# Attention in pairs of maps and modulation on two column tiles, in a two-layer diffusion trunk on one core

## The reference, cut to what matters

```python
mod = silu(c) @ w_mod[l] + b_mod[l]            # c and c_ctx; w_mod[l] is 1024 x 6144
shift1, scale1, gate1, shift2, scale2, gate2 = split(mod, 6)
h = rms_norm(x) * (1 + scale1) + shift1
q, k, v of three groups = h @ w_in[l]
#  A: 6 heads, window attention with a bias, plus context keys
#  B: 4 heads, two softmax maps each, p0 - lambda * p1
#  C: 6 query heads on 2 key heads
x = x + gate1 * (concat(softmax(q k) v) @ w_out[l])
h2 = rms_norm(x) * (1 + scale2) + shift2
x = x + gate2 * peer_ffn(h2)                   # 8 heads, top 16 of 16384 experts, for every token
```

## Time and profile before

| | |
|---|---|
| time, median of 3 runs | 5093.09 us (5086.49 to 5101.38) |
| the profiled execution | 5102.09 us, of it span 5100.3 us |
| PE busy | 75% of the span |
| DVE, ACT, POOL busy | 55%, 28%, 27% |
| mean granted TensorE clock | 0.924 |
| attention, layers 0 and 1 | 327.9 to 641.7 us, 2833.3 to about 3147 us |
| experts, layer 0 | 916.7 to about 2600 us |

### The profile page before, as it was taken

The page is one execution under the profiler, slowest core; times in us unless marked ns, Lnnn a source line. Parts: engine busy times, 40 slices in busy tenths (PEclk is TensorE's granted clock), DMA queues, the critical chain, the costliest instruction groups (busy, mean ns, idle before and its releaser), DMA issues.

```text
span 5100.3 us, 42883 instructions
## 1 busy us (share of the span) xinstructions
PE 3820.1 (75%) x14332; PEld 1753.3 (34%) x14332; DVE 2829.5 (55%) x6023; ACT 1444.8 (28%) x4223; POOL 1398.6 (27%) x1477
## 2 busy tenths in 40 slices
PE   7787779887777777777767776867777777777776
PEld 1364436222222222323234544432222222222222
DVE  2443365665675766745455334556657567575444
ACT  1224422222223222222222334222222222322222
POOL 1001200233343333433320111003333334333332
PEclk9886779999999999999988758989999999999999
DMA  7210012999999999999951000119999999999997
GB/s 253 72 40 1 1 54 73 389 407 406 417 414 416 416 406 413 401 416 401 418 188 50 15 1 17 63 68 410 412 412 416 411 419 406 420 416 395 406 419 290
DMA packets 214077, 1460.21 MB, mean 286 GB/s; under 512 B 23968, under 2 KB 24224, under 8 KB 49248
## 3 DMA queue, kind: packets, MB, share of 16 engines
q0 software_dynamic: 186496, 1355.11, 65.1%
q1 hardware_dynamic: 27360, 102.37, 5.9%
HBM read 1453.19 MB, written 4.19 MB: 286 GB/s over the span
## 4 chain that ended last, share of the span: by engine, by line
PE 41%; DMA 37%; DVE 12%; ACT 6%; issue 4%; SPq 0%; POOL 0%; ACTq 0%; DVEq 0%; POOLq 0%
DMA work<-expert_dram,work 29%; PE psum L656 17%; PE psum L448 10%; DMA hT<-expert_dram,work 7%; DVE work L1243 4%; PE psum L543 3%; PE psum L560 2%; PE psum L460 2%; PE psum L575 2%; ACT work L863 2%; PE psum L515 2%; DVE work L983 1%; ACT work L853 1%; ACT work L776 1%; PE psum L485 1%
## 5 line engine op out<-in xcount | busy, mean ns | idle before, releaser
L656 PE MATMUL psum<-work 128*128 128x512 f32 x3416 | 1606.1, 614 | 535.2 <-ACT work L863 535.2
L1243 DVE SCALAR_TENSOR_TENSOR work<-work,psum 128x1024 f32<-128x1024 f32 x854 | 1041.2, 1220 | 866.8 <-DMA work<-expert_dram,work 856.5
L1301 POOL DMA_INDIRECT work<-expert_dram,work x854 | 823.5, 964 | 1506.2 <-PE psum L656 1334.7
L656 PEld LDWEIGHTS psum<-work 128*128 128x128 f32 x3416 | 626.4, 193 | 1502.7 <-ACT work L863 866.5
L656 PE MATMUL psum<-hT,work 128*128 128x512 f32 x1704 | 810.1, 619 | 329.0 <-ACT work L863 329.0
L853 ACT ACTIVATE work<-work,xinv 128x2 f32<-128x2 f32 x640 | 189.1, 295 | 2390.5 <-DVE work L1243 1573.5
L1243 DVE SCALAR_TENSOR_TENSOR hT<-hT,psum 128x1024 f32<-128x1024 f32 x426 | 519.5, 1220 | 448.4 <-DMA hT<-expert_dram,work 448.1
L1301 POOL DMA_INDIRECT hT<-expert_dram,work x426 | 418.2, 982 | 864.0 <-PE psum L656 693.7
L656 PEld LDWEIGHTS psum<-hT,work 128*128 128x128 f32 x1704 | 315.0, 194 | 815.9 <-ACT work L863 496.3
L448 PE MATMUL psum<-hT,split 128*128 128x128 f16 (+1 forms) x2880 | 430.9, 310 | 58.0 <-DVE hT L1018 58.0
L863 ACT ACTIVATE work<-const,work 128x128 f32<-128x128 f32 x1280 | 434.1, 386 | 0.0
(11 more groups left out here) (152 smaller groups left out, 2771.3 us busy)
## 6 DMA issues: line engine op xcount, KB each, us to landing
ring<-w_mod_dram SPq DMA_DIRECT2D x96, 512.0 KB, 4.9
ring<-w_in_dram SPq DMA_DIRECT2D x40, 512.0 KB, 3.6
ring<-w_query_dram SPq DMA_DIRECT2D x32, 512.0 KB, 3.5
work<-expert_dram,work POOLq DMA_INDIRECT x854, 8.5
ring<-w_out_dram SPq DMA_DIRECT2D x16, 512.0 KB, 3.6
hT<-expert_dram,work POOLq DMA_INDIRECT x426, 8.5
work<-rpb_dram POOLq DMA_DIRECT2D x4, 1344.0 KB, 19.7
xT<-xT_dram SPq DMA_DIRECT2D x1, 2560.0 KB, 11.5
```

Source lines behind the costliest of these rows:

```text
L656: last = pe.matmul(out[:, cols_], diag[:, n % NDIAG, :], rows[n % NBUF][:, D + 512 * half:D + 512 * half + 512], start=(s == 0), stop=(s = ...
L1243: dve.scalar_tensor_tensor(u, u, 1.0, pair[t % 2], ALU.mult, ALU.mult, accum_out=act_in[:, s:s + 1]).then_inc(dot_done, 1)
L1301: pool.indirect_dma_start(rows[n % NBUF], None, a[f"expert{l}"], bass.IndirectOffsetOnAxis(expert[:, t % 2, s:s + 1], 0)).then_inc(row_in[ ...
```

## The change

It has two parts, and both are made at once.

Attention is worked off in steps k over pairs of maps (2k, 2k + 1). PE issues per step: S(k), V of the unit that ended with pair k - 2, then T of the items of pair k - 1. The transposes of a unit's first item go into `pair[2]`, those of the second into `pair[3]` (banks 6 and 7), so a T waits for the copy of the item before last. The output of V has one place, in bank 7, instead of two; the T that writes bank 7 waits for the copy of that output. ACT does per step: the output copy, then copy of the first turned item, exponential of 2k, copy of the second turned item, exponential of 2k + 1. DVE does both maxima, both inverses, then the mixing, which used to come after the next map's maximum. POOL's queue is as it was.

Modulation: a tile now holds 1024 output columns for one block of the contraction. Its two products go to different column tiles of PE (output partitions 0 and 1, and 32 and 33) and to different banks, 2 and 3. A chunk is eight tiles and 1024 outputs; it needs both banks, so its first tile waits until the chunk before is copied out. There are half as many chunks with two copies and eight transposes each. The results go to banks 4 and 5 (layer 0) or 6 and 7 (layer 1), and `project(0)` waits until DVE has read them. The bytes loaded, the number of products and the number of tiles ahead of the norm and of the experts (16 and 24) stay.

```diff
@@ def build
-        modps = psum[:, 7, 0:NMOD * 2].rearrange("p (m s) -> p m s", s=2)
+        modps = [[psum[:, bank + x, 0:NMOD].rearrange("p (c i s) -> p c i s", i=4, s=2) for x in range(2)]
+                 for bank in (4, 6)]
@@ PE def mod_tile
-                if q == 0 and NCHUNK * l + c >= 2:
-                    pe.wait_ge(mod_row, NCHUNK * l + c - 1)
-                w = ringx[:, n % RING, 0:KC * P]
-                for k in range(2):
-                    last = pe.matmul(psum[0:2, 2 + c % 2, :], cT[:, 2 * q + k, :], w[:, 512 * k:512 * k + 512],
-                                     start=(q == 0 and k == 0), stop=(q == 3 and k == 1))
+                if k == 0 and NCHUNK * l + c >= 1:
+                    pe.wait_ge(mod_row, NCHUNK * l + c)
+                for x in range(2):
+                    last = pe.matmul(psum[32 * x:32 * x + 2, 2 + x, :], cT[:, k, :],
+                                     ringx[:, n % RING, 512 * x:512 * x + 512], start=(k == 0), stop=(k == KC - 1))
@@ PE def project
+                if l == 0:
+                    pe.wait_ge(mod_read, 2)
@@ PE def attention
-                for n in range(NMAP + LAG_V):
...
+                for k in range(NPAIR + 2):
+                    n = 2 * k
+                    if k < NPAIR:
+                        if k > 0:
                             pe.wait_ge(exp_done, NMAP * l + n)
...
+                    u = pair_unit(k - 2)
+                    if u is not None:
                         it = ITEMS[UNITS[u]["last"]]
                         pe.wait_ge(pt_done, NITEM * l + UNITS[u]["last"] + 1)
-                        if u >= 2:
-                            pe.wait_ge(o_evac, NUNIT * l + u - 1)
+                        if u >= 1:
+                            pe.wait_ge(o_evac, NUNIT * l + u)
...
-                                last = pe.matmul(psum[64 * hh:64 * hh + 64, 6 + u % 2, 0:P], v,
+                                last = pe.matmul(psum[64 * hh:64 * hh + 64, 7, 2 * P:3 * P], v,
...
-                    if n - LAG_T in BY_LAST:
+                    for i in pair_items(k - 1):
...
-                        if i > 0:
-                            pe.wait_ge(pt_done, NITEM * l + i)
+                        if i > 1:
+                            pe.wait_ge(pt_done, NITEM * l + i - 1)
+                        if it["hh"] == 1 and u is not None:
+                            pe.wait_ge(o_evac, NUNIT * l + u + 1)
...
-                            last = pe.transpose(pair[2][:, b * P:(b + 1) * P], src[:, b * P:(b + 1) * P], con("ident"))
+                            last = pe.transpose(pair[2 + it["hh"]][:, b * P:(b + 1) * P], src[:, b * P:(b + 1) * P],
+                                                con("ident"))
@@ ACT def mod_copy
-                act.activation(mrow[l], psum[0:2, 2 + c % 2, :], ACT.Copy).then_inc(mod_row, 1)
+                for x in range(2):
+                    last = act.activation(mrow[l][x], psum[32 * x:32 * x + 2, 2 + x, :], ACT.Copy)
+                last.then_inc(mod_row, 1)
@@ ACT def attention
+                for k in range(NPAIR + 2):
+                    u = pair_unit(k - 2)
+                    if u is not None:
                         act.wait_ge(pv_done, NUNIT * l + u + 1)
                         tok = slice(UNITS[u]["t"] * P, (UNITS[u]["t"] + 1) * P)
-                        act.activation(oT[:, UNITS[u]["chunk"], tok], psum[:, 6 + u % 2, 0:P],
+                        act.activation(oT[:, UNITS[u]["chunk"], tok], psum[:, 7, 2 * P:3 * P],
                                        ACT.Copy).then_inc(o_evac, 1)
+                    turned = pair_items(k - 1)
+                    for x in range(2):
+                        if x < len(turned):
...
+                            act.activation(probT[:, it["unit"] % 2, it["hh"], 0:w], pair[2 + it["hh"]][:, 0:w],
+                                           ACT.Copy).then_inc(pt_done, 1)
+                        if k < NPAIR:
+                            n = 2 * k + x
...
+                            act.activation(prob[:, n % NPROB, 0:w], pair[x][:, 0:w], ACT.Exp,
@@ DVE def attention
-                for n in range(NMAP + 2):
-                    if n < NMAP:
+                for k in range(NPAIR):
+                    for n in (2 * k, 2 * k + 1):
...
+                    for n in (2 * k, 2 * k + 1):
+                        s = n % NPROB
+                        dve.wait_ge(exp_done, NMAP * l + n + 1)
                         dve.reciprocal(stat[:, 2, s:s + 1], stat[:, 1, s:s + 1]).then_inc(rinv_done, 1)
...
+                    for i in pair_items(k):
+                        it = ITEMS[i]
+                        if it["kind"] == "B":
...
+                            dve.wait_ge(scaled, NSCALED * l + SCALED[it["last"]] + 1)
+                            dve.scalar_tensor_tensor(prob[:, s0, 0:w], prob[:, s0, 0:w], stat[:, 2, s0:s0 + 1],
+                                                     prob[:, s1, 0:w], ALU.mult, ALU.add).then_inc(mixed, 1)
@@ def kernel
-    ins["w_mod"] = w_mod.reshape(L, 4, 2, P, NCHUNK, 512).transpose(0, 4, 1, 3, 2, 5).reshape(L, NMOD, P, KC, P)
+    ins["w_mod"] = w_mod.reshape(L, KC, P, NCHUNK, KC * P).transpose(0, 3, 1, 2, 4).reshape(L, NMOD, P, KC, P)
```

More of the change, by code:

```diff
@@ L118, with pair_items, pair_unit @@
 NMAP, NITEM, NUNIT = len(MAPS), len(ITEMS), len(UNITS)
+NPAIR = NMAP // 2
 BY_LAST = {it["last"]: i for i, it in enumerate(ITEMS)}
 UNIT_BY_LAST = {ITEMS[u["last"]]["last"]: i for i, u in enumerate(UNITS)}
+def pair_items(k):
+    return [BY_LAST[n] for n in (2 * k, 2 * k + 1) if n in BY_LAST] if 0 <= k < NPAIR else []
+def pair_unit(k):
+    return UNIT_BY_LAST.get(2 * k + 1) if 0 <= k < NPAIR else None
 SCALED = {m: i for i, m in enumerate([m for m, x in enumerate(MAPS) if x["kind"] != "B" or x["c"] == 1])}
@@ L260, in build @@
         sums = psum[:, 6, 256:256 + RING + 1]
-        modps = psum[:, 7, 0:NMOD * 2].rearrange("p (m s) -> p m s", s=2)
-        mrow = [work[0:2, 0:512], work[0:2, y_at - 512:y_at]]
+        modps = [[psum[:, bank + x, 0:NMOD].rearrange("p (c i s) -> p c i s", i=4, s=2) for x in range(2)]
+                 for bank in (4, 6)]
+        mrow = [[work[32 * x:32 * x + 2, at_:at_ + 512] for x in range(2)] for at_ in (0, y_at - 512)]
         def con(name, p=P):
@@ L468, in mod_turn @@
                     pe.wait_ge(mod_read, 1)
-                for i in range(4):
-                    last = pe.transpose(modps[:, 4 * c + i, :], mrow[l][:, i * P:(i + 1) * P], con("ident", 2)[:, 0:2])
+                for x in range(2):
+                    unit = const[32 * x:32 * x + 2, CO["ident"] + 32 * x:CO["ident"] + 32 * x + 2]
+                    for i in range(4):
+                        last = pe.transpose(modps[l][x][:, c, i, :], mrow[l][x][:, i * P:(i + 1) * P], unit)
                 last.then_inc(mod_turned, 1)
@@ L474, in mod_chunks @@
                 for c in range(lo, hi_):
-                    for j in range(4 * c, 4 * c + 4):
+                    for j in range(KC * c, KC * c + KC):
                         mod_tile(l, j)
@@ L758, in attention @@
             def attention(l):
-                for n in range(NMAP + LAG_V):
-                    if n < NMAP:
-                        m = MAPS[n]
-                        w = TOK if m["t"] < TT - 1 else NCTX
-                        act.wait_ge(max_done, NMAP * l + n + 1)
-                        if n >= NPROB:
-                            act.wait_ge(tr_done, NITEM * l + MAPS[n - NPROB]["item"] + 1)
-                        act.activation(prob[:, n % NPROB, 0:w], pair[n % 2][:, 0:w], ACT.Exp,
-                                       bias=stat[:, 0, n % NPROB:n % NPROB + 1],
-                                       accum_out=stat[:, 1, n % NPROB:n % NPROB + 1]).then_inc(exp_done, 1)
-                    if n - LAG_T in BY_LAST:
-                        i = BY_LAST[n - LAG_T]
-                        w = TOK if ITEMS[i]["t"] < TT - 1 else NCTX
-                        act.wait_ge(tr_done, NITEM * l + i + 1)
-                        u, hh = ITEMS[i]["unit"], ITEMS[i]["hh"]
-                        if u >= 2:
-                            act.wait_ge(pv_done, NUNIT * l + u - 1)
-                        act.activation(probT[:, u % 2, hh, 0:w], pair[2][:, 0:w], ACT.Copy).then_inc(pt_done, 1)
-                    if n - LAG_V in UNIT_BY_LAST:
-                        u = UNIT_BY_LAST[n - LAG_V]
@@ L834, in experts @@
                 if l + 1 < L:
-                    for c in range(MOD_EARLY - 2):
+                    for c in range(MOD_EARLY - 1):
                         mod_copy(l + 1, c)
@@ L838, in experts @@
                 if l + 1 < L:
-                    for c in range(MOD_EARLY - 2, MOD_EARLY):
-                        mod_copy(l + 1, c)
+                    mod_copy(l + 1, MOD_EARLY - 1)
                 for t in range(TT):
@@ L871, in _ @@
                 if l == 0:
-                    for c in range(FIRST_CHUNK + 3, NCHUNK):
```

(11 more changed lines are left out.)

66 lines of the change are left out of this document (32 added, 34 removed).

## The result

The kernel after the change takes 5128.21 us, the median of 7 runs (5114.58 to 5139.08), against 5093.09 us of the kernel before in the same 7 rounds (5086.49 to 5111.04). The ratio is 1.0062, with a 95% interval of 1.0047 to 1.0078: slower by some 32 us, as the ratio has it (the medians differ by 35). The forecast was 5132 us. The profiled execution of the kernel after took 5117.29 us, of it span 5115.5 us.

The account below looks back on a forecast made before the run. Attention was taken as bound by a chain of waits between engines, layer 0's modulation by PE. Attention +57, modulation -13 and -5 gave +39: 5132 us by the median, range 5108 to 5155, with rivals 1 and 3 5082 to 5166.

Parts of the forecast that it names:

- The line through attention: Attention step: S, V, T, copy, exponential, copy, exponential, next S in line; 6.25 us at full clock, 9.06 at half.
- B: Attention stretch with quarter-height scores and one item per pair: steps 6.13 us, 8.46 with V; +15 us a layer.
- A: Attention's first stretch, with a bias on DVE: steps 9.06 against 9.25 us at half clock, clock about unchanged; -2 us a layer.
- C and its clock: Attention's last stretch: +3.5 us a layer from longer steps less faster drain, +12 from granted clock falling to about A's.
- rival 1: Attention: C's clock stays at 0.88, so attention +33, in sum +15, 5108 us; chance 0.17.
- the walk: Adding instruction times along attention's line, per step; gave C 84 us all at full clock and 121 all at half.
- Rival 2: Attention: A and C are granted the full clock, so attention -16, with modulation -34, 5059 us; chance 0.12.
- Modulation, layer 0: First modulation stage: PE 0.87 us a tile, then transfers at 1.51 last, borders cost nothing; -13 us, between -17 and 0.
- Rival 3: Modulation: column tiles bring nothing, run in turn or lost to exposed copies; +12 instead of -18, 5162 us; chance 0.14.
- the Trainium skill's warning on evacuation: Modulation, layer 0: tiling speeds products, not their evacuation, so copies may limit; would take back at most 9 us.
- Modulation, layer 1: Tiles among layer 0's experts: first dot product 2.6 us earlier, transfers ahead of gathers; -5 us, ends -9 and +3.
- The sum: Whole kernel: attention +57, modulation -13 and -5, together +39 us; 5132 us in terms of the median.

Follow-up runs that it names:

- swap: Kernel after with only ACT's order edited: output copy first, then each exponential ahead of the copy beside it; 5022.19 us in one run.
- exp_first: Kernel after with both ACT exponentials of a step ahead of the copies, and bank 7's wait adapted; 4963.65 us, 0.9747 of the kernel before.
- att_only: New attention with the old modulation; 5131.37 us, 1.0074 of the kernel before.
- mod_quads: New modulation with the old attention, odd chunks on column tiles 64 and 96 to avoid waiting for the previous chunk's copies; 5079.14 us, 0.9969 of the kernel before.
- best: exp_first with the column tiles of mod_quads; 4949.61 us, 0.9728 of the kernel before.
- mix_late: Kernel after with DVE's mixing in B moved behind the next pair's maxima; 5160.2 us in one run.

## Why the prediction was right, and where its terms were off

**The line through attention: right.** Where a step runs at one clock it came out as walked: 9.04 us at half clock and 6.23 us at full against 9.06 and 6.25; in B 8.45 and 6.10 us against 8.46 and 6.13. V lost its wait and S got it, as foretold. `swap` edits nothing but ACT's order and the layer falls by 50 us; `exp_first`, with one wait of PE moved along, by 80 us. What the forecast lacked are the steps of A with a short V or T, at 5.37 us, where the maximum comes as late as the copies.

**B: right.** +13.8 us a layer against +15. Its clock went from 0.50 to 0.57, which the forecast did not have; the 1 us that is missing may be that.

**C and its clock: right in size.** +12.5 us a layer against +3.5 and +12. The end of the stage did drain 3 us faster. The clock of C did fall to about A's old one, 0.78, so rival 1 (C stays at 0.88) was wrong. The +12 for it follows from no sum: by the forecast's own figures of 84 and 121 us, half of the time at half clock gives 99 us (it has 98), 8 more than its 91, and 70% gives 16 more. If the 3.5 us hold, the clock's part was 9 us.

**A: the term that was mis-sized.** The forecast had -2 us a layer, and it was -9.4. It stands on "so A stays about where it was", that is at 0.76; A was granted 0.86. In the second layer of `att_only`, where A was granted 0.75, A took 106.0 us, 2.9 less than before, near the 2 foretold, and as the instructions are the same, the 6.5 us between its two layers are the clock's. That the sum comes near the walk there is partly luck, though: the third group's steps are 5.37, 7.33, 9.01, 7.85 and 4.52 us, where before they were 6.26, 6.60, 8.60, 8.37 and 4.43, and most of the 2.9 us lies in the first group, whose long steps went from 9.25 and 9.07 to 7.80 and 7.85 us. The walk had some 10 steps 0.2 us shorter, not steps that move by up to 0.9 us either way. Rival 2 asked for a clock near 1.00 in A and C; A's rose about halfway there, C's fell. Attention in sum is then +17 us a layer in the profiled execution, +34 in all against +57, and +38 in the runs of `att_only`.

**Modulation, layer 0: the rate on PE was right, transfers and borders were not.** The four instructions of a tile start 0.21 us apart, and a tile takes 0.86 us against 0.87 foretold. But where transfers are last, from the fifth tile on, a tile takes 1.60 us in `mod_quads` and 1.55 us in `best`, with 1.51 foretold: 1.2 to 2.5 us over 27 tiles. And the step "Up to four loads are under way meanwhile, so I cost it at nothing" put the borders too low: they cost about 2.6 us, half of what PE waits at them. The norm starts 2.6 us earlier on average, with 2 to 3 foretold, though the two traces with the old modulation lie 3.9 us apart. The tiles give 6.8 us (57.7 less 50.8) instead of 11, and `project(0)` starts 9.7 us earlier on average (130.7 against 140.4), where the forecast had 13; the profiled pair alone would say 8.3 (133.88 against 142.23). Rival 3, by which the tiles run one after the other, was wrong; the Trainium skill's warning on evacuation, which stood with it, holds in part: the copies took back 2.6 of the 9 us that were foretold as the most.

**Modulation, layer 1: right in kind, its size not settled.** Foretold was that DVE's first dot product would no longer wait for `turn_rows` but for the gather:

```profile
926.65 1.04 POOL L1325 DMA_INDIRECT work<-expert_dram,work  x1 [158.37 <-DVE work L1244]
...
929.54 1.09 PE L635 MATMUL psum<-const,work 128*128 128x128 f32 x8
...
935.88 1.22 DVE L1267 SCALAR_TENSOR_TENSOR work<-work,psum 128x1024 f32<-128x1024 f32 x1 [7.85 <-DMA work<-expert_dram,work]
```

From first gather to first dot product it is 9.23 us, where it was 11.43: 2.2 us less, with 2.6 foretold. Over all traces with either modulation it is 9.1 against 13.4 us on average, but only two have the old one, 4 us apart. The further 2.4 us for transfers out of the way can't be seen: from 960 to 1060 us the DMA share is 1.02 at 418 and 419 GB/s in the kernels before and after.

**The sum.** Attention +34 (+38 by `att_only`, 28 to 47) instead of +57, modulation -10 (3 to 16 less) instead of -18. Both terms were taken too large, and as they have opposite signs, part of the errors cancelled: +39 us was foretold, +28 is the sum of the two parts measured alone, and +35 is what the median of 5128.21 us stands above 5093.09. That the forecast of 5132 us lies 4 us from the median is in part such luck.

Two points remain open. What decides whether A is granted 0.86 or 0.75 with the same instructions is not settled. And from the first gather of layer 0 to the first S of layer 1, the six traces with the same modulation take 1903.0 to 1914.6 us, so a single profiled pair can't show a gain of a few us there. The two with the old modulation take 1916.6 and 1920.2 us, which would allow for more than the 5 us foretold; both are of runs above their median (5102.09 against 5093.09 and 5135.81 against 5131.37 us).

## What to carry to other kernels

In an in-order queue, put the instruction that releases the next round ahead of those whose inputs come out of this round: the same five ACT instructions in another order were worth some 160 us of 5128 here. Before costing a change of order, write the line of instructions that stand in each other's way from one round's start to the next, at each clock; it gave the times of steps at one clock to 0.03 us. A second buffer that the forecast held to be worth nothing in one order was worth 78 us in another, so cost it again after each change of order. And before reading a few us off one pair of traces, look at every trace that has the same code in that stage: here six of them spread a 50 us stage over 4.6 us, and the one profiled pair would have doubled the price of the borders.

## What the runs showed of the hardware

The granted clock of PE is not a function of the instructions alone. The same A stage was granted 0.86 in both layers of the kernel after, and 0.86 and 0.75 in the two layers of `att_only`, with 99.5 and 106.0 us; each pattern then held for the second and third group of its layer. `mix_late` shows both once more, at 106.0 and 99.5 us. The Trainium skill (TensorE: Matmul & The Clock Gate, What's actually happening) says that the count of slow products at a kernel's start varies from run to run; these rows show such a choice held on to for some 60 us in the middle of a kernel.

The clock can also fall where PE gets faster. Modulation ran at 1.00 before, with no pauses on PE; in the kernel after, with pauses for transfers and borders, it was granted 0.88 and 0.76. The same borders don't bring this about each time: `exp_first`, with the same modulation, was granted 1.00 in the same stretch, and so was `mod_quads`, which has none of the waits. The views by stretch, of the kernel after, of `exp_first` and of `mod_quads`:

```profile
97.00:111.00 14.00, 9.69 (x40) 1.49 (x40) 1.56 (x2) 2.41 (x4) 0.00 (x0) 0.88 0.88 290
111.00:125.00 14.00, 10.40 (x32) 1.30 (x32) 0.85 (x1) 0.59 (x2) 0.00 (x0) 0.76 0.82 295
```

```profile
97.00:111.00 14.00, 9.89 (x48) 1.38 (x44) 1.56 (x2) 2.03 (x4) 0.00 (x0) 1.00 0.92 336
```

```profile
97.00:111.00 14.00, 8.99 (x42) 1.17 (x44) 0.00 (x0) 1.17 (x2) 0.00 (x0) 1.00 0.94 346
```

What decides between them was not found.

And weights of two columns in neighbouring column tiles, with 32-bit operands, overlap fully here: at full clock four instructions take 0.86 us, where in one column tile they took 0.44 us each.
